# Two transformer blocks: convolution input in four products, diagonals made ahead, unseen keys left out

## The reference, cut to what matters

```python
proj = rms_norm(x, norm1_g) @ w_in + b_in          # 1024 a, 1024 gate, 1024 q, 128 k, 128 v
h = a * sigmoid(gate)                               # 1024 channels
h = causal depthwise convolution of 31 taps + bias  # per channel
conv_out = silu(layer_norm(h))
q, k = per-head norm and partial rotary             # 16 heads of 64, 2 key heads
scores = q k^T / 8 over the own and the previous block of 128 keys
mask = (kpos <= qpos) & (qpos - kpos < 128) & (kpos >= 0)
probs = exp(scores - m) / (sum + exp(sink - m)),  m = max(scores, sink)
x = x + concat(conv_out, probs v) @ w_out
x = x + peer(rms_norm(x, norm2_g), ...)             # 16384 experts, gated
```

## Time and profile before

| what | value |
|---|---|
| median of three runs | 3358.91 us (3358.5 to 3361.52) |
| profiled execution, its own time | 3359.69 us |
| span in its trace | 3357.9 us |
| PE busy | 3266.8 us, 97% |
| DVE busy | 2255.3 us, 67% |
| ACT busy | 1555.1 us, 46% |
| mean granted clock of TensorE | 0.993 |

### The profile page before, as it was taken

One profiled execution on the slowest core, in us unless ns is written; L12 is line 12 of the kernel. 1 busy time (PEld: TensorE's weight loads), 2 busy tenths in 40 slices (PEclk: granted clock), 3 DMA queues, 4 the chain that ended last, 5 costly groups with the idle time before them and its releaser, 6 DMA issues.

```text
span 3357.9 us, 52739 instructions
## 1 busy us (share of the span) xinstructions
PE 3266.8 (97%) x20942; PEld 2882.6 (86%) x20942; DVE 2255.3 (67%) x3198; ACT 1555.1 (46%) x1986; POOL 5.6 (0%) x14
## 2 busy tenths in 40 slices
PE   8999999999999999898799999999999999999999
PEld 6999998788888888886689999888788888888887
DVE  5664455676576566688668997568778577865554
ACT  4554344555355455445544444443444444435353
POOL 0000000000000000000000000000000000000000
PEclk9999999999999999999999999999999999999999
DMA  6445565565655655552255554554555555555654
GB/s 229 160 147 195 188 203 188 177 198 189 193 180 194 195 188 182 165 171 75 73 193 167 164 176 146 176 177 152 181 181 177 188 187 178 182 188 188 194 188 165
DMA packets 161252, 590.50 MB, mean 176 GB/s; under 512 B 17904, under 2 KB 18064, under 8 KB 159728
## 3 DMA queue, kind: packets, MB, share of 16 engines
q1 hardware_dynamic: 160192, 583.14, 53.5%
q0 software_dynamic: 816, 3.98, 0.3%
HBM read 584.96 MB, written 2.10 MB: 175 GB/s over the span
## 4 chain that ended last, share of the span: by engine, by line
PE 90%; DVE 7%; ACT 2%; issue 1%; DMA 0%; DVEq 0%; SPq 0%; ACTq 0%
PE PS L407 19%; PE PS L366 12%; PE PS L368 12%; PE PS L367 12%; PE PS L410 9%; PE PS L376 7%; PE PS L377 7%; PE PS L378 7%; DVE LO L292 2%; PE PS L1352 1%; PE PS L1363 1%; DVE GB L987 1%; PE PS L591 0%; PE PS L662 0%; ACT UN L618 0%
## 5 line engine op out<-in xcount | busy, mean ns | idle before, releaser
L292 DVE TENSOR_TENSOR LO<-RAW,HI 128x1024 fp32r<-128x1024 f32 x1096 | 1327.2, 1218 | 811.3 <-ACT HI L291 808.7
L291 ACT ACTIVATE HI<-RAW 128x1024 fp32r<-128x1024 f32 x1096 | 1150.2, 1055 | 1208.7 <-PE PS L368 621.7
L407 PE MATMUL PS<-XX,HI 128*128 128x512 f32 x2688 | 736.2, 395 | 0.0
L376 PE MATMUL PS<-XX,HI 128*128 128x256 f32 x2176 | 622.9, 286 | 12.0 <-DVE LO L292 9.6
L377 PE MATMUL PS<-XX,HI 128*128 128x256 f32 x2176 | 615.5, 283 | 0.0
L378 PE MATMUL PS<-XX,LO 128*128 128x256 f32 x2176 | 615.4, 283 | 0.0
L366 PE MATMUL PS<-HI,FH 128*128 128x512 f32 x1504 | 593.2, 394 | 5.3 <-DVE FL L533 4.9
L368 PE MATMUL PS<-HI,FL 128*128 128x512 f32 x1504 | 586.3, 390 | 0.0
L367 PE MATMUL PS<-LO,FH 128*128 128x512 f32 x1504 | 585.2, 389 | 0.0
L407 PEld LDWEIGHTS PS<-XX,HI 128*128 128x128 f32 x2688 | 460.1, 189 | 61.9
L410 PEld LDWEIGHTS PS<-XX,LO 128*128 128x128 f32 x2688 | 412.5, 189 | 57.2
(11 more groups left out here) (253 smaller groups left out, 2335.5 us busy)
## 6 DMA issues: line engine op xcount, KB each, us to landing
RAW<-in_peer_v SPq DMA_DIRECT2D x256, 512.0 KB, 3.9
RAW<-in_ffn_w_up SPq DMA_DIRECT2D x176, 512.0 KB, 4.0
RAW<-in_peer_ut_rest SPq DMA_DIRECT2D x160, 512.0 KB, 4.0
RAW<-in_w_in SPq DMA_DIRECT2D x136, 512.0 KB, 3.7
RAW<-in_peer_ut SPq DMA_DIRECT2D x96, 512.0 KB, 3.6
RAW<-in_ffn_w_down SPq DMA_DIRECT2D x88, 512.0 KB, 4.1
RAW<-in_w_mix_out SPq DMA_DIRECT2D x32, 512.0 KB, 4.3
RAW<-in_w_in_2c SPq DMA_DIRECT2D x32, 512.0 KB, 4.2
```

The source lines that it names most:

```text
L291: hi_done.append(AC.do(lambda e, raw=raw, hi=hi: e.activation(hi, raw, ACT.Copy), landed[i], used))
L292: lo_done.append(DV.do(lambda e, raw=raw, hi=hi, lo=lo: e.tensor_tensor(lo, raw, hi.bitcast(F32), ALU.subtract), hi_done[i], landed[i], used))
L376: e.matmul(o, h, x, start=f, stop=False, skip_group_check=True)
L407: e.matmul(o, hi[:, k, w], XX[:, 4 * u + k, :, :].rearrange("p h s -> p (h s)"), start=u == 0 and k == 0, stop=False, skip_group_check=True)
```

## The change

The convolution input becomes four products. The host puts the columns of `w_in_2c` in another order, so that product `p` holds the values of channel blocks 2p and 2p+1 and their gates side by side. The taps of blocks 0 and 1 are queued after the first product, those of 2 and 3 after the second; then come q, k and v, and then the third and the fourth product. Blocks 4 and 5 get four taps a step. The 31 diagonals of block 6 are made ahead, in two background generators of two a step: 16 into the memory of `STAGE` beside q, 15 into `UF` after the biases there have been read; the second takes the place of `pause(8)`. `causal_pe` is one generator for both blocks; from its ninth matmul on it makes one diagonal a matmul, 23 ahead. `attention` is told how many key blocks each query block sees: (2, 2) in the first block of the network, which leaves its work as it was, and (1, 2) here.

```diff
-    add_units("w_in_2c", [2, 0])
+    add_units("w_in_2c", [0, 1])
     add_units("w_in_2q", [0, 1])
     add_units("w_in_2kv", [0], 256)
-    add_units("w_in_2c", [3, 1])
+    add_units("w_in_2c", [2, 3])
...
         def score(qt, g):
+            n = 128 * seen[qt]
...
-                        m = e.matmul(b[:, 256 * j:256 * j + 256], qt_[64 * r:64 * r + 64, h, 128 * qt:128 * qt + 128],
-                                     kt_[64 * r:64 * r + 64, h // per, :], start=True, stop=True,
+                        m = e.matmul(cols[:, j, :], qt_[64 * r:64 * r + 64, h, 128 * qt:128 * qt + 128],
+                                     kt_[64 * r:64 * r + 64, h // per, 0:n], start=True, stop=True,
...
-                m = AC.do(lambda e, h=h: e.activation(sc[:, h, :], sc[:, h, :], ACT.Exp, bias=ng[:, h:h + 1],
+                m = AC.do(lambda e, h=h: e.activation(sc[:, h, 0:n], sc[:, h, 0:n], ACT.Exp, bias=ng[:, h:h + 1],
...
         def turn_over(qt, g):
-            for kb in range(2):
+            for kb in range(seen[qt]):
...
+    def diagonal(c, k):
+        n = len(diagonals) % 32
+        d = DG[n // 16][:, n % 16, :]
+        diagonals.append((d, n, AC.do(lambda e: e.activation(d, ident, ACT.Copy, scale=par("cw2", 31 * c + k)),
+                                      dg_read[n])))
+
+    def build(c, ks):
+        for k in ks:
+            diagonal(c, k)
+            if k % 2:
+                yield
+
+    def causal_pe(cs, m_h):
+        for c in cs:
+            i, b, fr = spare()
+            held.add(i)
+            for k in range(31):
+                at = 31 * (c - cs[0]) + k
+                if at >= 8 and len(diagonals) < 31 * len(cs):
+                    diagonal(cs[len(diagonals) // 31], len(diagonals) % 31)
+                d, n, m = diagonals[at]
+                dg_read[n] = m = PE.do(lambda e, c=c, k=k, d=d, b=b: e.matmul(
+                    b[:, 0:S], d, HP[:, c, k:k + S], start=k == 0, stop=k == 30, skip_group_check=True),
                     m, m_h, m_pad, fr if k == 0 else None)
+                if k % 4 == 3:
+                    yield
...
+    def conv_input(p, m_h):
         pair, banks, m = product(False, 16, XH, XL, x_ready)
+        m_sg = [AC.do(lambda e, c=c, b=banks[1]: e.activation(
+            SG[:, (2 * p + c) % 4, :], two(b)[:, c, :], ACT.Sigmoid, bias=par("b2", 8 + 2 * p + c)), m, m_h,
+            arena_free) for c in range(2)]
+        acc_free[pair] = m_h = [DV.do(lambda e, c=c, b=banks[0]: e.scalar_tensor_tensor(
+            out=HP[:, 2 * p + c, 30:286], in0=two(b)[:, c, :], scalar=par("b2", 2 * p + c),
+            in1=SG[:, (2 * p + c) % 4, :], op0=ALU.add, op1=ALU.mult), m, m_sg, arena_free) for c in range(2)]
         return m_h
 
     m_h = conv_input(0, None)
-    beside.append(causal([0, 1, 2, 3], m_h, 3))
+    beside.append(causal([0, 1], m_h, 3))
+    m_h = conv_input(1, m_h)
+    beside.append(causal([2, 3], m_h, 3))
+    background.append(build(6, range(16)))
...
     m_bi_read = free
+    dg_read[16:] = [m_bi_read] * 16
...
     beside.insert(0, together(heads_normed(0), heads_normed(1)))
-    background.append(pause(8))
+    background.append(build(6, range(16, 31)))
     background.append(attention(2, Z2[:, :, 0:1024], KD2, V2, QT2, KT2, sc2, PT2, const("mask2"), SINK[:, 1, :], 8,
-                                m_qk, box2, False))
-    m_h = conv_input(1, m_h)
+                                m_qk, box2, (1, 2)))
+    m_h = conv_input(2, m_h)
+    beside.append(causal([4, 5], m_h, 4))
+    m_h = conv_input(3, m_h)
     m_x_read = mm_done[-1]
-    beside.append(causal([4, 5], m_h, 3))
-    on_pe = [causal_pe(c, m_h) for c in (6, 7)]
+    on_pe = [causal_pe((6, 7), m_h)]
```

More of the change, by code:

```diff
@@ L537, in two, with attention @@
         return b.rearrange("p (c s) -> p c s", c=2)
-    def attention(nkv, q_tok, k_tok, v_tok, qt_, kt_, sc, pt, mask, sink, at0, m_in, res_box, on_pool):
+    def attention(nkv, q_tok, k_tok, v_tok, qt_, kt_, sc, pt, mask, sink, at0, m_in, res_box, seen):
         per = 8 // nkv
@@ L586, in score, with fn @@
                 i, b, fr = spare()
-                def fn(e, r=r, b=b):
+                cols = b[:, 0:2 * n].rearrange("p (h k) -> p h k", k=n)
+                def fn(e, r=r, cols=cols):
                     for j in range(2):
                         h = 2 * g + j
-                        m = e.matmul(b[:, 256 * j:256 * j + 256], qt_[64 * r:64 * r + 64, h, 128 * qt:128 * qt + 128],
-                                     kt_[64 * r:64 * r + 64, h // per, :], start=True, stop=True,
+                        m = e.matmul(cols[:, j, :], qt_[64 * r:64 * r + 64, h, 128 * qt:128 * qt + 128],
+                                     kt_[64 * r:64 * r + 64, h // per, 0:n], start=True, stop=True,
                                      skip_group_check=True)
@@ L596, in score @@
                 m = PE.do(fn, fr, m_q, m_k)
-                d = s4[:, 2 * g:2 * g + 2, r, :]
-                mk = mask[:, 256 * qt:256 * qt + 256].unsqueeze(1).to_broadcast([128, 2, 256])
-                t_free[i] = DV.do(lambda e, b=b, d=d, mk=mk: e.tensor_tensor(d, two(b), mk, ALU.add), m, m_turn,
+                d = s4[:, 2 * g:2 * g + 2, r, 0:n]
+                mk = mask[:, 256 * qt:256 * qt + n].unsqueeze(1).to_broadcast([128, 2, n])
+                t_free[i] = DV.do(lambda e, cols=cols, d=d, mk=mk: e.tensor_tensor(d, cols, mk, ALU.add), m, m_turn,
                                   turned[g])
                 m_add.append(t_free[i])
-            m_mx[qt].append(DV.do(lambda e: e.tensor_reduce(mx[:, 4 * g:4 * g + 4], sc[:, 4 * g:4 * g + 4, :], AX.X,
+            m_mx[qt].append(DV.do(lambda e: e.tensor_reduce(mx[:, 4 * g:4 * g + 4], sc[:, 4 * g:4 * g + 4, 0:n], AX.X,
                                                             ALU.max), m_add, m_in))
@@ L625, in divide @@
             rd = stats[qt][4]
+            n = 128 * seen[qt]
             for h in range(4 * g, 4 * g + 4):
-                m_div[g] = AC.do(lambda e, h=h: e.activation(sc[:, h, :], sc[:, h, :], ACT.Copy,
+                m_div[g] = AC.do(lambda e, h=h: e.activation(sc[:, h, 0:n], sc[:, h, 0:n], ACT.Copy,
                                                              scale=rd[:, h:h + 1]), m_rd[g])
@@ L659, in fn @@
                     for r in range(2):
-                        for kb in range(2):
+                        for kb in range(seen[qt]):
                             rhs = pt[:, kb, 2 * h0:2 * h0 + 2 * per, :].rearrange("p (h r) s -> p r h s", r=2)[:, r]
                             m = e.matmul(b[64 * r:64 * r + 64, c:c + 128 * per], v_tok[:, kb, 64 * kv:64 * kv + 64],
-                                         rhs, start=kb == 0, stop=kb == 1, skip_group_check=True)
+                                         rhs, start=kb == 0, stop=kb == seen[qt] - 1, skip_group_check=True)
                 return m
@@ L749, in _program @@
     background.append(attention(4, q_tok, k_tok, V1, QT, KT, sc1, pt1, const("mask1"), SINK[:, 0, :], 0,
-                                [m_rope[-1], free], box1, False))
+                                [m_rope[-1], free], box1, (2, 2)))
     CT = GB[:, 0:1024].rearrange("p (c s) -> p c s", c=4)
@@ L992, in causal @@
                     yield
[L994 to L1013, removed]
-            yield
[L1015 to L1022, removed]
@@ L1024, in conv_input @@
-    def conv_input(half, m_h):
-        pair, banks, m = product(False, 16, XH, XL, x_ready)
[L1027 to L1033, removed]
+    DG = [z[:].rearrange("p c s -> p (c s)")[:, 0:2048].rearrange("p (i j) -> p i j", j=128) for z in (STAGE, UF)]
@@ new lines, in _program @@
+    dg_read = [m_down] * 32
+    diagonals = []
+    def diagonal(c, k):
[19 more added lines that the diff above has]
+                    b[:, 0:S], d, HP[:, c, k:k + S], start=k == 0, stop=k == 30, skip_group_check=True),
+                    m, m_h, m_pad, fr if k == 0 else None)
+                if k % 4 == 3:
+                    yield
+            m_cv[c] = t_free[i] = DV.do(lambda e, c=c, b=b: e.tensor_scalar(CV[:, c, :], b[:, 0:S], par("cb2", c), None,
+                                                                           ALU.add), m, m_res)
+            held.discard(i)
+            yield
@@ L1577 @@
         "w_in_2kv": _units(w2[:, 3072:], 256),
-        "w_in_2c": _units(w2[:, :2048]),
+        "w_in_2c": _units(np.concatenate([w2[:, a:a + 256] for p in range(4) for a in (256 * p, 1024 + 256 * p)], axis=1)),
         "w_out_2": _units(g["w_out_2"]),
```

## The result

The changed kernel takes 3338.64 us in the median (3337.04 to 3339.88, 4 runs), the kernel before 3360.22 beside it: ratio 0.9935, interval 0.9918 to 0.9953, 21.6 us less. The prediction was 3341 in a range of 3328 to 3354. The profiled execution spans 3337.5 us, 20.4 less than before.

What follows compares the result with a forecast made beforehand. TensorE bounds nearly everywhere except the tail after the last product, where engines wait in turn or ScalarE sets the pace. Tail and leftover -24.2, ahead of it +6.2, net -18 on 3358.91: 3341 us, range 3328 to 3354.

Steps and rivals of the forecast that it cites:

- The leftover taps: After the tail, 36 taps delay the next weight unit's split; with none left over, the whole 7.8 us goes.
- The first query block: First part of attention after the head: VectorE becomes the fuller engine, 29.7 us plus some 4 waiting; 38.4 falls to 34.
- Rival A: In-order queues set both query blocks, which keep their pace; only head and leftover are won: 3353 us, chance 0.14.
- rival B: Query blocks fall to 30 and 24, near their fullest engine, and the new wait costs 3: 3331 us, chance 0.13.
- The second query block: Last part of the tail: ScalarE's chain loses 23 diagonals, 6.7 us, and gains 1.4; 31.9 falls to 26.6.
- the term for longer taps: In the second query block, half of the longer taps adds 1.4 us to ScalarE's chain.
- Keys left out: First query block keeps 128 of 256 keys: 3.3 us of ACT saved, half-width score pairs and maxima on DVE.
- The costs ahead of the tail: Before the last product ends: 1.3 for diagonals, 3.4 for earlier attention, 1.5 for clock, together +6.2 us.
- the early step: Attention starts one step earlier, in the fourth product; PE waits 5.4 us for normalised keys: +3.4, and 1.5 for clock.
- ScalarE's diagonals: Fifteen diagonals built while the heads are normalised, where ACT is already late: 1.3 us of PE added (0 to 2.6).
- The clock: After the new wait for keys the array is throttled and matmuls run slower: 1.5 us added (0 to 3).
- Rival C: VectorE bounds the products, in the second convolution product and q, PE waiting at 24 units: 3365 us, chance 0.04.

Runs made afterwards that it cites:

- The order alone: Kernel before with only the order of products and taps changed (four products, three taps a step): 3354.22 us against 3361.08, ratio 0.998.
- the late run: Changed kernel with one more empty step ahead of the second attention, so its first transposes come a unit later: 3339.33 us, ratio 0.9939.

## Why the prediction was right

*The leftover taps.* Counted to go, and gone: 17.0 became 8.9. The order alone brought 6.9 us, most of the 7.8.

*The first query block.* Right in size and cause: 33.8 for 34, DVE 29.7 busy for a sum of 29.7, ACT 21.3 for 21.1, and 3.5 us of waiting for the first exponentials where some 4 were counted. (Nine rounds of 1.58 are 14.2, not the 14.6 of the sum; it moves the result by 0.4.) The three lengths at four, three and two taps show that VectorE sets it. Rival A, hand-overs, falls with them for this block; so does the part of B that asked for less than VectorE's own time.

*The second query block.* The cause is shown by the run with no diagonals ahead: 6.6 us more than the late run, for the 6.7 of the forecast, though at different clocks (0.90 and 0.82). The gain was sized too small, 5.3 for a measured 7.1; 24.8 us is nearer to the 24 of rival B. Of the 1.8 us, 0.7 are the term for longer taps, put at 1.4: with three taps in place of four the block is 24.1 instead of 24.8, and its value matmuls wait twice 1.06 us for VectorE's copies, not twice 1.45. Where the other 1.1 us come from is not shown.

*Keys left out.* A half-width exponential takes 0.39 us, the diagonal's figure, as the forecast took it. The Trainium skill (VectorE: DVE Perf Modes, The TRN2 errata) says that each SBUF operation pays a fixed cost besides that of its elements; 0.39 us for half of what took 0.494 agrees. The maximum at half width took 0.69 for the 0.65. Together the keys left out are worth 6.8 us.

*The costs ahead of the tail.* Forecast 6.2, measured 6.3, and in part that is luck: the early step cost 5.5 for 3.4 and 1.5, ScalarE's diagonals 1.2 for 1.3, and 0.4 us less that nobody counted (48.8 with sixteen diagonals, 49.2 before) make up for it. The wait is 5.39 for 5.4 because the diagonals delay PE and the keys by the same 1.2 us. That these costs count as a pure loss was too simple: with the late attention PE has 5.5 us less ahead of the tail, and the total does not move with four taps and falls by some 2 us with three.

*The clock.* The 1.5 us were taken from one row of before. After the 5.39 us wait PE is slow from 1519.6 to 1523.6, 4.0 us at 0.50, of which half, 2.0 us, are lost. With 2.0 in the place of 1.5 the early step comes to 5.4 of its 5.5. The Trainium skill (TensorE: Matmul & The Clock Gate, HAM oscillation) says that an idle gap throttles the array, so that the matmuls behind it run slowly. The trace agrees for this wait.

*Rival C.* PE was busy for all of the 23.0 us in the second convolution product and of the 22.5 us in the first product of q; VectorE, with 18.6 and 20.6 us, fits.

The median fell by 3.6 us more than the 18 forecast: 1.8 are the second query block, 0.8 the head, and the rest lies within the spread of the runs.

What stays open is how much of the time of a tail is its clock. The late run, the one with sixteen diagonals and the order alone all show a lower clock (0.80 to 0.85) in parts of the tail than the kernel before (0.96 and 1.00), each in one profiled execution; no run held the clock fixed. The mean clocks of whole runs point the same way: 0.992 to 0.993 in the five runs of the late kernel, 0.993 to 0.994 in the four of the changed one.

## What to carry to other kernels

Where several generators share in-order queues, count the calls: which generator's step falls behind which matmul, and what is left over after the last one, give most of the result before any duration is known. In a stretch where no engine is full, add up the work of each engine by part; the fullest sum plus its first wait was right to a microsecond, and one tap less a step moved it as the sum says, until TensorE was nearly full as well. A wait that a change adds is a loss only as far as nothing was bought with it; test it by moving the waiting step back alone, and test it again when the work behind it changes: here the wait cost nothing with four taps a step and some 2 us with three.

## What the runs showed of the hardware that was not expected

The clock granted to PE differs between kernels of nearly the same work: in the second query block it was 1.00 before, 0.93 after, 0.82 with the late attention, 0.80 with sixteen diagonals ahead and 0.90 with none. Where it is low, matmuls on the path double: the same eight records of the values took 3.62 us in one run and 1.94 in another. It can differ behind the same wait, too. In the second query block of the kernel before and of the one with the order alone, PE comes to eight diagonal records after the same wait of 3.10 us for ScalarE; they take 1.99 us in the first and 3.78 in the second, where the granted clock from there to 1606.0 is 0.50:

```profile
1599.85 1.99 PE L1017 MATMUL PS<-HP,STAGE 128*128 128x256 f32 x8 [3.10 <-ACT STAGE L1008]
```

```profile
1602.20 3.78 PE L1017 MATMUL PS<-HP,STAGE 128*128 128x256 f32 x8 [3.10 <-ACT STAGE L1008]
```

Kernels also differ in how far their executions lie apart: with no diagonals ahead the five runs lie between 3341.79 and 3347.77 us, with late attention and three taps within 2.3 us. The spread goes with the clock: with no diagonals ahead the mean granted clock is 0.994 in the runs of 3341.79 and 3341.92 us, 0.992 in those of 3345.09 and 3345.47, and 0.991 in that of 3347.77. What lowers it in one execution and not in the next is not shown.
